# The gather of three pairs ahead moved behind the scatter and the extra tile's transfers in GpSimd's loop of the expert stage

## The reference, cut to what matters

```python
hf = rmsnorm_2(x, ffn_norm)                      # (256, 1024)
...
g_idx = argmax(g_logits)                         # 1 of 4 groups
top_v, top_i = lax.top_k(e_in, 2)                # 2 of its 8 experts
...
for g in range(4):
    a = jnp.einsum('nd,edf->nef', hf, w_gate[g]) # d = 1024, f = 256
    u = jnp.einsum('nd,edf->nef', hf, w_up[g])
    act = jax.nn.silu(a) * u * combine[:, g, :, None]
    out = out + jnp.einsum('nef,efd->nd', act, w_down[g])
```

## Time and profile before

| | |
|---|---|
| median of 3 runs | 1679.57 us (1677.57 to 1680.19) |
| the profiled execution: its time | 1677.86 us |
| its span in the profile | 1676.2 us |
| TensorE busy | 1552.3 us (93%) |
| GpSimd busy | 151.8 us (9%) |
| mean granted TensorE clock | 0.972 of full speed |
| gathers of rows, from issue to landing | 6.8 us least, 9.4 median, 11.9 most |

### The profile page before, as it was taken

How to read it: one execution, slowest core, us unless ns; L and a number is a source line. 1 busy time by engine, 2 the same in 40 slices (tenths; PEclk the granted TensorE clock), 3 DMA queues, 4 the chain that set the end, 5 groups by cost and what they waited for, 6 DMA issues and landing times.

```text
span 1676.2 us, 23054 instructions
## 1 busy us (share of the span) xinstructions
PE 1552.3 (93%) x9664; PEld 1253.1 (75%) x9664; DVE 915.1 (55%) x1298; ACT 761.6 (45%) x1201; POOL 151.8 (9%) x202
## 2 busy tenths in 40 slices
PE   7999999999999999997999998989999999686676
PEld 6888888788887888875788888977999977333332
DVE  5545577745464554567644545796876765510102
ACT  6444554544364444466644444556755653111111
POOL 0000000100010000011100001050001000232320
PEclk9999999999999999999999999999999999798988
DMA  7555545555557455532345554432553248999996
GB/s 290 176 188 189 201 164 178 187 179 193 181 178 269 169 177 185 191 126 101 137 178 188 189 177 160 151 126 101 176 174 104 101 176 325 369 415 413 414 416 274
DMA packets 55366, 347.23 MB, mean 207 GB/s; under 512 B 10516, under 2 KB 10916, under 8 KB 15168
## 3 DMA queue, kind: packets, MB, share of 16 engines
q1 hardware_dynamic: 47520, 333.17, 53.8%
q0 software_dynamic: 7744, 12.61, 2.2%
HBM read 396.34 MB, written 9.96 MB: 242 GB/s over the span
## 4 chain that ended last, share of the span: by engine, by line
PE 78%; DVE 8%; DMA 7%; ACT 4%; issue 3%; POOL 1%; SPq 0%; DVEq 0%; POOLq 0%; ACTq 0%
PE A L424 31%; PE Y L454 20%; PE A L377 6%; PE A L362 4%; PE A L2985 4%; DMA raw<-experts,extra 2%; PE Y L3006 2%; DMA raw_whi<-experts 2%; DVE wlo L322 1%; PE A L438 1%; PE Y L393 1%; DMA raw<-stream 1%; ACT whi L311 1%; PE A L721 1%; DVE xn L521 1%
## 5 line engine op out<-in xcount | busy, mean ns | idle before, releaser
L322 DVE TENSOR_TENSOR wlo<-raw,whi 128x2048 fp32r<-128x2048 f32 (+1 forms) x226 | 496.9, 2206 | 246.2 <-ACT whi L311 245.3
L311 ACT ACTIVATE whi<-raw 128x2048 fp32r<-128x2048 f32 (+1 forms) x226 | 415.7, 1848 | 93.1 <-DMA raw<-stream 93.1
L424 PE MATMUL A<-whi,xh 128*128 128x512 f32 x768 | 308.5, 402 | 5.1 <-DVE wlo L322 5.1
L424 PE MATMUL A<-whi,xl 128*128 128x512 f32 x768 | 301.4, 392 | 0.0
L424 PE MATMUL A<-wlo,xh 128*128 128x512 f32 x768 | 300.8, 392 | 0.0
L424 PEld LDWEIGHTS A<-whi,xh 128*128 128x128 f32 x768 | 144.9, 189 | 34.2 <-DVE wlo L322 5.9
L424 PEld LDWEIGHTS A<-whi,xl 128*128 128x128 f32 x768 | 144.6, 188 | 31.7
L424 PEld LDWEIGHTS A<-wlo,xh 128*128 128x128 f32 x768 | 145.1, 189 | 28.4
L454 PE MATMUL Y<-whi,hh 128*128 128x512 f32 x352 | 140.8, 400 | 1.2 <-DVE hl L801 1.2
L454 PE MATMUL Y<-wlo,hh 128*128 128x512 f32 x352 | 139.4, 396 | 0.0
L454 PE MATMUL Y<-whi,hl 128*128 128x512 f32 x352 | 139.3, 396 | 0.0
(11 more groups left out here) (464 smaller groups left out, 2791.1 us busy)
## 6 DMA issues: line engine op xcount, KB each, us to landing
raw<-stream SPq DMA_DIRECT2D x216, 1024.0 KB, 4.9
raw_whi<-experts SPq DMA_DIRECT2D x39, 1024.0 KB, 26.5
raw<-experts SPq DMA_DIRECT2D x22, 1024.0 KB, 28.5
far<-experts SPq DMA_DIRECT2D x17, 1024.0 KB, 18.7
raw_x<-experts SPq DMA_DIRECT2D x12, 1024.0 KB, 28.5
xn<-experts SPq DMA_DIRECT2D x6, 1024.0 KB, 28.3
gains<-post_rows POOLq DMA_DIRECT2D x6, 512.0 KB, 4.7
far<-sums_at SPq DMA_DIRECT2D x4, 512.0 KB, 5.8
```

The source lines that it names most:

```text
L311: nc.scalar.activation(whi[:, n % RING, c], raw[:, n % RING, c], ACT.Copy).then_inc(hi_ready.sem, 1)
L322: nc.vector.tensor_tensor(wlo[:, n % RING, c], raw[:, n % RING, c], whi[:, n % RING, c].bitcast(F32), ALU.subtract).then_inc(lo_ready.sem, 1)
L424: ins = nc.tensor.matmul(bank, lhsT=lhs[:, kk, tok(t)], rhs=w[:, k, :], start=(kk == 0 and q == 0), stop=(kk == KD - 1 and q == 2))
```

## The change

In each step of GpSimd's loop the gather of pair q + 3 stands last instead of first. The waits inside each function are the same, and no instruction is added or taken away.

```diff
                 for q in range(PAIRS):
-                    if q + 3 < PAIRS:
-                        gather(q + 3)
                     if 0 <= q - 1 < SENT:
                         scatter(q - 1)
                     if q == 1:
                         weights(0)
                     elif q in extra_pairs[:-1]:
                         weights(extra_pairs.index(q) + 1)
+                    if q + 3 < PAIRS:
+                        gather(q + 3)
```

## The result

| | before | with the change |
|---|---|---|
| median | 1677.57 us (1674.35 to 1680.19, 5 runs) | 1688.41 us (1687.65 to 1692.83, 5 runs) |
| span of the profiled execution | 1676.2 us | 1686.7 us |

The ratio is 1.0067, with a 95% interval of 1.0053 to 1.0082: the change costs 10.8 us by the medians. The forecast was 1689 us, in a range of 1680 to 1697.

A forecast was written before the change was run, and what follows sets the result against it. The chain of extra pairs' weight issues on GpSimd was taken as the bound, with the end 45.8 us after the last. 5.9 + 6.6 - 1.5 - 0.6 = 10.4 us gave 1688.3 or 1690.0; stated 1689 us, range 1680 to 1697.

The forecast's parts named there:

- pair 4's gather: second weight issue: Start of the expert stage: pair 4's gather lands at 1474.4 us, so the next weight issue comes 5.9 us later.
- first interval over three pairs: Between extra weight issues: pair 7's gather lands late, so 21.1 us becomes 27.7, 6.6 more.
- third and fifth: Later intervals between weight issues, over three pairs: 29.2 and 28.3 us become 27.7, 1.5 and 0.6 less.
- the three over two pairs: Short intervals between weight issues: unchanged at 23.1, 21.9 and 22.7 us, covered by the weight transfers' own landing.
- last weight issue to the end of the span: End of the stage: the span ends 45.8 us after the last weight issue, unchanged.
- the clock: TensorE's half pair behind a late gather's wait: a slower clock adds 1.6 us once per wait.
- The floors of the fourth and sixth weight issue: The stream's own times for these issues, 1557.53 and 1607.67 us; the new times would lie above them.
- the stream would have no hole: SyncE's weight queue, some ten transfers deep: a delay of 6 to 11 us eats a part, nothing lost.
- That the stream absorbs it: Expert stage: late gathers only eat slack TensorE had in waiting for weights; 1678 to 1682 us, chance 0.18.
- The longer wait on both kinds of interval: Intervals between weight issues: gathers land in 11.9 us, slow clock in short ones too; 1698 us, chance 0.08.
- That the scatter gains: GpSimd's loop: an earlier scatter helps if `leave` waited for it; up to 4 us, 1675 us, chance 0.04.
- The page's rule: Gather landing by the cited page: 2.6 us for 256 KB, so the change would cost nothing; chance 0.01.

The follow-up runs named there:

- four-buffer run: Changed order, with a fourth buffer for the rows and the gather of four pairs ahead instead of three: 1677.13 us, ratio 1.0001.
- half-stream runs: Reloaded expert weights of ordinary pairs cut to half their columns, in the changed kernel and in the kernel before: 1647.08 and 1645.26 us.
- two-ahead run: Changed order, with the gather of two pairs ahead instead of three: 1762.32 us, ratio 1.0499.
- first fill: Changed kernel with 64, 56, 60 and 46 idle transposes on TensorE ahead of the rows of pairs 4, 7, 12 and 17: 1691.69 us.
- pair 4 restored: Changed kernel with only the gather of pair 4 put back ahead of the first scatter: 1684.69 us, ratio 1.0053.

## Why the prediction was right

The mechanism was right: late gathers of four extra pairs, waited for by TensorE, three long intervals alike, the short ones unchanged. The total fits to 0.1 us of the profiled span (1686.6 forecast, 1686.7 measured), and that is luck: counted from the stage's first gather the last weight issue moved by 14.1 us, not 10.4, and two terms that the forecast didn't have, -2.3 and -1.4, brought it back. Point by point:

| step | forecast | measured |
|---|---|---|
| pair 4's gather: second weight issue | +5.9 | +7.2 |
| first interval over three pairs | +6.6 | +7.2 |
| third and fifth | -1.5, -0.6 | -0.7, -0.4 |
| the three over two pairs | 0 | -0.3, +0.7, +0.4 |
| last weight issue to the end of the span | 0 | -2.3 |
| the stage's start, in these two executions | - | -1.4 |
| sum | +10.4 | +10.5 |

**The bound.** That the end hangs on the extra pairs' weight issues, and not on the stream alone, is borne out by the chain of waits and by the runs with only some gathers late: a delay of 7 us that the stream's pace could take back cost nothing, and the same delay with long intervals of 28 us behind it cost 4.2 us of the last weight issue, and 0.14% of the time by the two ratios (1.0067 against 1.0053, intervals that overlap).

**The sizes.** The gathers landed in 10.4, 9.6, 10.0 and 8.6 us where the forecast had 11.2 once and 9.5 three times: right on the whole, and 0.8 us too long for pair 4, which hid a part of the next error. The term that was too small is the clock. It was put at 1.6 us a wait, from one half pair; measured against the earlier trace rows, turn, half and down together took 3.0 us more behind pair 4's wait (1.11, 3.57 and 2.37 us) and 2.0 behind pair 7's. The two runs with TensorE kept busy took back 2.1 and 2.7 of the first. Of the 7.2 us in the first row 0.7 lie ahead of the first weight issue and belong to the spread of that part. The floors of the fourth and sixth weight issue lay under the new times, as said. That the stream would have no hole was wrong: its share fell to 0.87 from 1580 to 1590 us and to 0.85 from 1630 to 1640, and SyncE, which waits for places to come free, issued nothing from 1574 to 1588 us and from 1624 to 1639. The chain that ended last has no transfer of SyncE's weights in it, so this cost nothing that it shows.

**The end.** The forecast carried the 45.8 us behind the last weight issue over unchanged. It became 43.5, and another chain ended last. Before, it was the last scatter and the reading back of the sums, 7.00 and 4.45 us. After, in order of time:

```profile
1677.43 1.98 PE Y L3006 x16
...
1679.44 0.61 ACT yt L3054
...
1680.09 1.15 PE A L3015 x4
...
1681.34 1.29 DVE h L3117 x2
```

TensorE's merge of the last pair ends last; the stream was over by then, from 1660 to 1670 us only 26 GB/s were moved, and SyncE could issue the reading back at 1669.26, 3.7 us behind the last scatter's issue (1665.58) instead of 7.1. Behind the last extra weights' landing the clock also rose a little sooner: turn and half took 0.44 and 1.86 us there, where before they took 0.85 and 2.20. The four-buffer run shows the same from the other side: counted from the first gather, its last weight issue came 2.5 us sooner than before, and the end 0.4 us later. The rule "end is last weight issue plus 45.8" holds only near where it was read.

**The rivals.** That the stream absorbs it was the right picture for a single late gather and the wrong one for four. Its point of decision, a landing of about 7 us, fits the half-stream runs, where gathers that landed in 5.8 us or less cost nothing in the long intervals, though the pauses named above gave them 2.8 us more. The longer wait on both kinds of interval didn't come: the short ones stayed within 0.7 us, and the chain has the weight transfers' landing in each of them. That the scatter gains was not seen: in neither kernel's trace does `leave` wait for one.

**The page's rule.** The Trainium skill, "DMA: Bandwidth & Descriptors", section on the anatomy of one DMA on the gpsimd path, has 2.0 us plus bytes over 436 GB/s, an estimate of 2.6 us for a gather of 256 KB. Under the full stream the traces disagree, with 6.9 to 11.1 us from pair 4's gather on in the changed kernel. Where less is moved beside it they come near: pair 4's gather with half the stream, beside 208 GB/s, landed in at most 3.3 us, and the last gather of the two-ahead run, issued at 1733.12 us beside 82 GB/s, in 3.3. The 256 KB are an upper bound: rows that a tile doesn't have are not moved, and the four late gathers all belong to empty extra pairs.

## What to carry to other kernels

A prefetch's distance is counted in what stands between its issue and its use on the issuing engine, waits included: moving a gather behind a scatter was free here, and behind a scatter, a wait for another engine's product and two transfers it made an interval of 21 us one of 28. Take its landing from the trace under the load that it will meet, since a gather took 3.3 us or near 10 here by what was moved beside it and stood ahead of it on its queue. And before adding up late transfers, ask what paced the stretch before: a single delay ahead of a stretch with slack vanished, and four of them used the slack up and more.

## What the runs showed that I had not expected

An extra pair's weights are out of bounds for every row here, so its transfers bring nothing, and yet they take 9.0 us to land beside the full stream and 4.4 beside half of it. They stand in the chain of every short interval. Whether they read HBM for nothing is open: the profile's page counts 396.34 MB read against 347.23 MB moved, 49.1 MB more, and with half the stream 356.49 against 307.40, again 49.1; the 16 transfers of 128 x 6144 fp32 would be 50.3 MB. No run leaves them out.

With the first fill, with half the stream, with pair 4 restored and in the other runs with ratios near 1, but not in the two kernels compared, some half pairs run in groups of a few matmuls with pauses of 0.3 to 0.8 us for which the profile shows no releaser, 4.6 us instead of 1.7. Most often it is the half pair just ahead of the turn of pair 7, 12 or 17. That made the fill's end hard to place, shortened the waits for rows in the run with pair 4 restored, and is a part of the 22.4 us in both half-stream kernels. Its cause stays open.
